# A two-layer hybrid decoder trunk: the first layer's modulation on TensorE instead of VectorE, with its loads in another order

## What is computed

```python
c_act = jax.nn.silu(c)
for l in range(DEPTH):
    mod = c_act @ ada_w[l] + ada_b[l]
    sh_m, sc_m, g_m, sh_f, sc_f, g_f = jnp.split(mod, 6, axis=-1)
    h = _rmsnorm(x, norm_mix_g[l]) * (1.0 + sc_m[:, None]) + sh_m[:, None]
    cols = h @ w_in[l]
    y_a = diff_attention(...); y_b = rwkv7_time_mix(...); y_c = forgetting_attention(...)
    mix = jnp.concatenate([y_a, y_b, y_c], axis=-1) @ w_out[l]
    x = x + g_m[:, None] * mix
    h = _rmsnorm(x, norm_ffn_g[l]) * (1.0 + sc_f[:, None]) + sh_f[:, None]
    x = x + g_f[:, None] * peer_ffn(h, peer_wq[l], peer_subkeys[l], peer_u[l], peer_v[l])
return _rmsnorm(x, final_norm_g)
```

## Time and profile before

| | us |
|---|---|
| median of 3 runs | 1841.66 (1837.55 to 1845.47) |
| the profiled execution: its time | 1839.77 |
| its span, first to last instruction | 1837.9 |
| busy: PE, DVE, ACT, POOL | 1314.2, 1398.9, 663.5, 517.6 |
| mean granted TensorE clock, as a share of 2.4 GHz | 0.851 |
| read from HBM | 703.64 MB; up to 421 GB/s in a slice |
| first dot product with a gathered row | 285.0 |

### The profile page before, as it was taken

How to read it: one execution, slowest core, us unless ns; L and a number is a source line. 1 busy time by engine, 2 the same in 40 slices (tenths; PEclk the granted TensorE clock), 3 DMA queues, 4 the chain that set the end, 5 groups by cost and what they waited for, 6 DMA issues and landing times.

```text
span 1837.9 us, 26377 instructions
## 1 busy us (share of the span) xinstructions
PE 1314.2 (72%) x9588; PEld 769.6 (42%) x9588; DVE 1398.9 (76%) x3327; ACT 663.5 (36%) x1634; POOL 517.6 (28%) x564
## 2 busy tenths in 40 slices
PE   2768787787877866787877867787877865555554
PEld 2657675453544534453444534443544531111111
DVE  5878588999974747999965748999965769985554
ACT  2313114444832233445732135336732233231112
POOL 2110012232332222232323232232422233343331
PEclk9875688897998987898988978898988977777777
DMA  9993669998999998999999999998999999999996
GB/s 393 421 396 139 229 240 403 401 415 352 361 420 421 421 420 355 383 414 367 400 421 421 420 420 372 393 422 339 378 421 421 421 421 420 404 405 421 421 421 261
DMA packets 97010, 706.42 MB, mean 384 GB/s; under 512 B 10992, under 2 KB 11504, under 8 KB 13296
## 3 DMA queue, kind: packets, MB, share of 16 engines
q0 software_dynamic: 80640, 587.24, 78.6%
q1 hardware_dynamic: 16240, 117.50, 15.7%
HBM read 703.64 MB, written 1.05 MB: 383 GB/s over the span
## 4 chain that ended last, share of the span: by engine, by line
DVE 43%; DMA 28%; PE 18%; issue 6%; ACT 4%; POOL 0%; DVEq 0%; ACTq 0%; POOLq 0%
DMA ringmem<-in_peer_uv_dram,eidx 23%; DVE ringmem L1451 15%; PE psum L785 5%; DMA W<-in_w_groups_dram 3%; PE psum L661 3%; PE psum L420 2%; DMA ringmem<-in_ada_pairs_dram 2%; DVE coef L1464 2%; DVE ringmem L1095 1%; PE psum L648 1%; DVE cand L1166 1%; DVE cand L1168 1%; DVE eid L1169 1%; DVE attn L1237 1%; DVE ast L1238 1%
## 5 line engine op out<-in xcount | busy, mean ns | idle before, releaser
L785 PE MATMUL psum<-ringmem,diag 64*64 64x512 f32 x4096 | 612.6, 724 | 280.8 <-ACT diag L1066 280.5
L387 POOL DMA_INDIRECT ringmem<-in_peer_uv_dram,eidx x512 | 492.0, 961 | 1082.3 <-PE psum L785 967.6
L1451 DVE SCALAR_TENSOR_TENSOR ringmem<-ringmem,psum 128x1024 f32<-128x1024 f32 x512 | 613.1, 1219 | 240.7 <-DMA ringmem<-in_peer_uv_dram,eidx 227.4
L785 PEld LDWEIGHTS psum<-ringmem,diag 64*64 64x64 f32 x4096 | 151.8, 154 | 605.8 <-ACT diag L1066 399.9
L1066 ACT ACTIVATE diag<-K,coef 128x128 f32<-128x128 f32 x512 | 176.5, 393 | 259.3 <-DVE coef L1464 258.9
L1058 ACT ACTIVATE coef<-dots 128x2 f32<-128x2 f32 x256 | 52.0, 203 | 509.9 <-DVE ringmem L1451 509.2
L420 PE MATMUL psum<-hT,W 128*128 128x128 f32 x1344 | 183.8, 298 | 40.4 <-DMA W<-in_w_groups_dram 22.1
L420 PEld LDWEIGHTS psum<-hT,W 128*128 128x128 f32 x1344 | 172.8, 210 | 83.5 <-issue 39.3
L1095 DVE SCALAR_TENSOR_TENSOR ringmem<-ringmem,diag 128x1024 f32<-128x1024 f32 x96 | 115.5, 1223 | 23.6 <-DMA ringmem<-in_ada_pairs_dram 21.4
L661 PE MATMUL psum<-hT,W 128*128 128x128 f32 x1024 | 126.1, 280 | 7.1 <-ACT hT L835 7.1
L661 PEld LDWEIGHTS psum<-hT,W 128*128 128x128 f32 x1024 | 120.1, 195 | 22.3 <-issue 12.2
(11 more groups left out here) (243 smaller groups left out, 1599.9 us busy)
## 6 DMA issues: line engine op xcount, KB each, us to landing
ringmem<-in_ada_pairs_dram POOLq DMA_DIRECT2D x48, 1024.0 KB, 18.4
W<-in_w_pieces_dram SPq DMA_DIRECT2D x48, 1024.0 KB, 9.4
W<-in_w_groups_dram SPq DMA_DIRECT2D x24, 1536.0 KB, 11.6
W<-in_w_groups_dram SPq DMA_DIRECT2D x12, 1024.0 KB, 9.7
ringmem<-in_peer_uv_dram,eidx POOLq DMA_INDIRECT x512, 14.9
W<-in_w_groups_dram SPq DMA_DIRECT2D x4, 1040.0 KB, 9.2
attn<-in_subkeys_t_dram SPq DMA_DIRECT2D x4, 1024.0 KB, 9.4
K<-in_consts_dram SPq DMA_DIRECT2D x1, 1546.0 KB, 18.3
```

The lines of the kernel that those rows point to most:

```text
L387: nc.gpsimd.indirect_dma_start(slot(k), None, rows, bass.IndirectOffsetOnAxis(ap=eidx[:, ph % 2, m:m + 1], axis=0)).then_inc(row_landed[q ...
L785: mm = nc.tensor.matmul(acc_part(r, half), diag[d, k % DIAGS, d], slot(k)[d, D + half * 512:D + (half + 1) * 512], start=(k % SEL == 0), s ...
L1451: ins = v.scalar_tensor_tensor(out=u, in0=u, scalar=1.0, in1=hrep, op0=ALU.mult, op1=ALU.mult, accum_out=dots[:, j:j + 1])
```

## The change

The first layer's modulation is computed on PE: `c` as a column, silu on ACT, 32 times side by side as the stationary operand, times rows of `ada_w` as the moving one. The 6144 outputs are three groups (`ADA_GROUPS`) of 2048, each eight slots of 128 inputs by 2048 outputs. A slot is four matmuls of 512 columns, each on 32 columns of the array and into 32 partitions of one PSUM bank. After eight slots ACT copies the bank (`ada_copy`), PE turns it with four transposes (`ada_turn`) and DVE adds the bias (`modulation`). The second layer's modulation stays on DVE, now in 24 slots of two chunks ("pairs"), all from segment 29 on. `lead_order` says where each slot stands on both engines.

The three other edits: SP waits for the seventh slot, not the sixth, before the first weights, and loads `c` for all partitions after the constants. POOL waits, ahead of slot 12, for the sixth projection (dq). POOL waits, ahead of the fourth gather, for the query of the fifth head.

```diff
+def lead_order():
+    rows = [(g, k) for g in range(ADA_GROUPS) for k in range(KD)]
+    pairs = [(None, n) for n in range(ADA_PAIRS)]
+    out = []
+    for seg in range(SEGMENTS):
+        for queue, n in ((rows, 3 if seg == 0 else KD - 3 if seg == 1 else seg % 7 == 6 if seg <= 28 else 1),
+                         (pairs, 0 if seg <= 28 else 1 if seg <= 44 else seg % 4 == 0 if seg <= 56 else 2)):
+            for _ in range(n):
+                if queue:
+                    out.append((seg,) + queue.pop(0))
+    return out
...
-                sp.wait_ge(row_landed[5], 16)
+                sp.wait_ge(row_landed[6], 16)
...
-                for q in range(ADA_SLOTS):
+                for q, (_, g, k) in enumerate(LEAD):
+                    n = ADA_GROUPS * KD + k if g is None else KD * g + k
+                    if q == 12:
+                        pool.wait_ge(s["proj_out"], at("proj_out", 0, 6))
...
+                    if k == 3:
+                        pool.wait_ge(s["q_out"], PH - 3)
...
+                def ada(q, g, k):
+                    if k == 0 and g >= 2:
+                        pe.wait_ge(s["ada_copied"], g - 1)
+                    if q == 0:
+                        pe.wait_ge(s["c_ready"], 1)
+                    pe.wait_ge(row_landed[q % RING], 16 * (q // RING + 1))
+                    for b in range(4):
+                        mm = nc.tensor.matmul(bank[g % 2][32 * b:32 * b + 32, :], ccol[:, k:k + 1].broadcast_to([P, 32]),
+                                              ringmem[:, q % RING, b * 512:(b + 1) * 512],
+                                              start=(k == 0), stop=(k == KD - 1), skip_group_check=True)
+                    mm.then_inc(slot_free[q % RING], 1)
+                def ada_turn(g):
+                    pe.wait_ge(s["ada_copied"], g + 1)
...
+                    for j in range(4):
+                        tr = nc.tensor.transpose(bank[2 + g % 2][:, j * P:(j + 1) * P], ada_row[:, j * P:(j + 1) * P], ident)
+                    tr.then_inc(s["ada_turned"], 1)
...
+                lead = Pace(mixing(0))
+                for q, (seg, g, k) in enumerate(LEAD):
+                    lead.upto(seg)
+                    if g is not None:
+                        ada(q, g, k)
...
-                for j in range(ADA_CHUNKS):
-                    ada(j)
...
-                    if j >= 2 * KD - 1:
-                        lead.upto(LEAD[j])
+                for q, (seg, g, k) in enumerate(LEAD):
+                    lead.upto(seg)
+                    if g is None:
+                        ada(q, k)
+                    if q == KD - 1:
+                        modulation(0)
+                    elif q - 2 in GROUP_END[1:]:
+                        modulation(GROUP_END.index(q - 2))
+                modulation_next()
```

133 lines of the change are left out of this document (76 added, 57 removed).

## The result

The changed kernel takes 1857.66 us (median of four runs, 1854.47 to 1861.28) against 1841.06 before (1837.55 to 1845.47): ratio 1.009, 95% interval 1.0058 to 1.0122. It is slower, by 16.6 us, and outside the range that I gave. The profiled execution has a span of 1853.3 us, 15.4 more than before.

The account below looks back on a forecast made before the run. Only the lead before the first gathered row was taken to change, with DVE the bound where the moved work lands. -10.4 (start, projections) + 11 + 2.2 (attention) - 1.6 + 0.5 = +1.7 on 1841.7 gave 1843 us, range 1831 to 1856.

Parts of the forecast that it names:

- (a): Projections: DVE has no products there any more, so PE's waits for DVE fall from 3.5 to about 0.5 us.
- (b): Projections: with POOL stopped until the sixth projection, r, v, fv, dq load nearly alone; 1.0 us of wait left for r.
- (c): Projections: after POOL's release the last three weight groups share again; dv's wait falls 4.0 to 2.6 us, fk's is 5.4.
- (d): Projections: with shorter waits PE is less often at half clock, -3.3 us (0 to -7).
- (e): Projections: PE takes four slots of the second group, 0.9 us each with tiles side by side, +3.6 us (to +16).
- (f): Attention: DVE has a pair of products in place of one in each of twelve steps, +11 us.
- (h): The four steps behind: pairs fill DVE's gaps, 1.3 us, and four transposes on PE cost 0.9; +2.2 us.
- (g): Attention: PE gets a slot in each of twelve steps; full clock and no cost assumed.
- (j): State sums to second norm: DVE loses six products' time, of which two stood in the way, -1.6 us.
- (k): Queries: five last pairs come first; first expert numbers 0.6 us later, second head's 7 earlier, neither setting the first row.
- (l): Gathers from the fourth on wait for the fifth query; the third may lose a microsecond; no cost.
- the half clock: Rival, chance 0.15: attention stays at half clock, PE outlasts DVE in its steps, +7 us, so 1850.

Follow-up runs that it names:

- e4: Changed kernel without GpSimd's wait for the projections ahead of the thirteenth slot: 1864.3 us, 1.0121 to the kernel before.
- e3: Changed kernel with DVE taking the turned sums of the modulation two slots later: 1855.29 us, 1.0061 to the kernel before.
- e2: Changed kernel without GpSimd's wait for the fifth query ahead of the fourth gather: 1859.62 us, 1.0103 to the kernel before.
- f3: Changed kernel with GpSimd's wait ahead of the fourth gather for the seventh query, not the fifth: 1850.92 us, 1.0054 to the kernel before.
- i2: Changed kernel with one more GpSimd wait, ahead of the seventh gather for the sixth query: 1851.43 us, 1.0053 to the kernel before.
- j3: Changed kernel with turned sums taken two slots later and the fourth gather behind the seventh query: 1844.45 us, 1.0027 to the kernel before.
- g3: Changed kernel, pairs spread with six in attention, turned sums later, slots from the thirteenth asked behind the second projection, three in flight: 1841.5 us, 1.0001 to the kernel before.
- g4: Changed kernel, pairs spread with five in attention, turned sums later, thirteenth slot behind the third projection without limit: 1838.25 us, 0.9973 to the kernel before.
- j1: Changed kernel, pairs spread with four in attention, eight behind step 56, turned sums later, thirteenth slot behind the fourth projection: 1833.56 us, 0.9956 to the kernel before.

## Why the prediction was wrong

I gave 1843 and 1831 to 1856; it is 1857.7, against a median before that hardly moved.

**Start**: +0.9 forecast, +0.8 measured. **(a), (b), (c)**: waits for weights of 9.0 us at dv and fk, 0.5 for DVE. Measured 9.5 us in five waits, of which 4.67 is the start's own; inside the stage 4.8, and not where I put them: dv waits for nothing, fq 2.6, fk 1.2; one wait for DVE, 1.3. The waits fall by 15.0 us and not by 11.6. The hold does more than I reckoned; e4 shows it to be worth some 5 us. **(d)** the clock: fk's thirty-two instructions take 3.84 us in place of 5.97, and over the stage PE is busy 61.3 us, of which some 4 are the four slots, in place of 63.5, at a clock of 0.93 in place of 0.88. So the same work is some 6 us cheaper, where I took 3.3. **(e)** the price of a slot on PE is right, 1.07 us at full clock and 1.93 at half: the tiles run side by side. Together the projections shrank from 85.6 to 66.8 us, 7.5 more than forecast; 1.0 of that is only moved, for the fourth slot stands between the projections' end and attention.

**(f), (h)** attention: +13.2 forecast, +19.5 measured (79.0 against 59.5). The pairs' part is about right: without the two waits for the transposes it is 73.1 (e3), +13.6, where 12.3 of the forecast were the pairs. The step that failed here is (h), where I took the transposes to cost their own 0.9 us. They cost 5.9, because DVE reaches the take before PE, which is a step behind, has even begun its slot. **(g)** the clock was 0.56 in the first half of attention and 0.78 in the second, not 1.00 (before: 0.58 in 124 to 154, 0.50 in 154 to 184). That was forecast wrongly, but the slots still lay for the most part beside DVE's work: no more than the 1.3 us between +13.6 and 12.3 is left for them. **(i)** held: DVE never waited for a slot in attention.

**(j), (k)**: from attention to the first query 57.9 us against 59.8, forecast 1.6 less. The first gather goes out 0.9 us later than before (267.3 against 266.4), of which 0.7 is the first query's; for the order of the pairs I had forecast 0.6.

So up to the first query the sum said +1.7 and the trace says +0.7, through errors of -7.5 and +6.3, and the 1.0 of that slot, that cancel. That is luck, and partly this trace's own early projections. The step that put the time out of the range is **(l)**, "No cost". I weighed whether the wait for the fifth query delays the gathers, found it harmless, and e2 confirms it. I did not ask what the gathers do to the heads once the ring is free and nine can go at once: +9.0 us between the first query and the first row, 6.1 of them at the sixth head and 2.8 at the seventh, whose query begins at half clock behind the hole. In the kernel before DVE freed the last slot only at 280.4, and eight gathers went out in the time of nine. f3 and i2 show that the hole needs the burst, and give 6.9 and 5.6 us of that stretch back by stopping GpSimd in it. Why the burst of the kernel before does no harm, and that of j3, stays open, and with it the mechanism.

The last 5 us came where I wrote that I would be wrong altogether if it changed. It did, by a little, and I have no cause for it.

Of the rivals the half clock came true in part, without its 7 us; the ring did not starve; the last weights came nearly in time, 3.8 us of waits in place of 8.0, which is part of the 7.5; no rival had the hole. The slower side had one mechanism too few: I looked for what a transfer may wait for, and not for what issuing it may hold up.

## What to carry to other kernels

When work moves off an engine, look where the rest of it lands: sixteen pairs in the stage where DVE sets the pace made it some 14 us longer, and the same change with four there, the others where DVE waits and the turned sums taken two slots later is faster than the kernel before by 0.7%. An operation that takes another engine's result must be placed by that engine's progress, not by its own order: two slots later made attention 5.9 us shorter. Half idle DMA queues beside a chain of double-buffered weights were not spare room here (e4, g3, g4, j1).

## What the hardware showed unexpectedly

In eight kernels a matmul's semaphore came 6.0 to 6.3 us late by the pace of the heads before it, while GpSimd was issuing gathers about every 1.25 us; with GpSimd stopped after six, 1.8 us; with three issued, in time. Eight gathers with three longer issues among them (1.96, 1.52, 1.44 us) did no harm, nor did six at full pace in j3. And a wait on GpSimd that held nothing where it stood (e2) took 6.9 us out of the stretch to the first row when moved by two queries (f3).
